# Moving two pairs of SBUF buffers by 192 bytes in a two-block transformer kernel

## The chip, the cores and the metric

The kernel is one program on one core of a Trainium2 chip. The metric is device time in microseconds (us) of one execution; lower is better. The times given are medians of several executions.

## The reference

Two transformer blocks work on 256 tokens of width 1024, in float32. The first has a gated feed-forward (inner width 2816), a mixer with two branches (a spatial gating unit and a stick-breaking attention of 16 heads), and a second gated feed-forward. The second has two attention layers, each followed by an MLP of inner width 4096. Nearly all arithmetic is the product of a 256-row activation with a weight that is streamed once from HBM:

```
def swiglu(x, w_gate, w_up, w_down):
    return (jax.nn.silu(x @ w_gate) * (x @ w_up)) @ w_down
...
def squared_relu_mlp(x, w_up, w_down):
    return jnp.square(jax.nn.relu(x @ w_up)) @ w_down
...
        h = h + merge_heads(mix) @ w_o[layer]
        h = h + squared_relu_mlp(rms_norm(h, mlp_norm[layer]), w_up[layer], w_down[layer])
```

## The kernel before

**Weights.** SyncE issues all weight loads in a fixed order, in units of 128 x 1024 (or 128 x 512) floats, into the ring `raw` (6 slots). For each unit ScalarE writes a rounded copy `w_hi` (L633) and VectorE the remainder `w_lo` (L985), both of type float32r, in rings of 8 slots. TensorE multiplies three times for one product: low activation by high weight, high by high, high by low (the helper `three`, L1479).

**Activations.** They are split in the same way. `xt` holds the normalized input, transposed, with high and low parts interleaved; `yt_hi`, `yt_lo` hold the attention outputs and other 1024-wide operands; `ht_hi`, `ht_lo` hold the inner activations of a feed-forward chunk. The chunks of a feed-forward alternate: even ones use `ht`, odd ones use `yt` (`h_buffers`).

**Two forms of matmul.** In the first (the up projections at L1568, L1570, L1575, and the projections to queries and keys at L1479) the weight is loaded as the stationary operand and `xt` is streamed, 256 columns. In the second (the down projections and all products that leave rows of tokens, L1479) the activation is loaded as the stationary operand, 128 columns, and the weight is streamed, 512 columns. Each matmul has its own weight load (LDWEIGHTS, "PEld" in the profile), which TensorE does while the matmul before it streams. `yt` and `ht` are only ever loaded as stationary operands in the second form; the one exception is the stick-breaking attention, where `ht` holds a triangular cumulative sum's input and is streamed (L1712, L1715).

**Where buffers lie.** SBUF tensors are placed one behind another in each partition. A filler `gap_in` of 192 bytes stands ahead of `xt`, and a filler `gap_out` of 64 bytes behind `ht_lo`. All the sizes between are multiples of 256 bytes, so modulo 256 the starts are: `raw`, `w_hi`, `w_lo`, `x`, `side` at 128; `xt`, `yt`, `ht` at 64; `work`, `qt`, `kt`, `vn`, the constants at 128. Every operand's offset inside its buffer is a multiple of 512 bytes for the matmuls of the two forms. So, modulo 256, in the second form the streamed weight starts 64 bytes past the stationary activation, and in the first form the streamed `xt` starts 192 bytes past the stationary weight.

**Order.** Each engine's instructions are written out by hand and joined by semaphores. The lines the prediction speaks of are these:

```
        gap_in = sb("gap_in", [P, 48])
        xt = sb("xt", [P, KT, 2, S], F32R)
...
        yt_hi = sb("yt_hi", [P, KT, S], F32R)
...
                for n, (p, q) in enumerate(((a[1], b[0]), (a[0], b[0]), (a[0], b[1]))):
                    ins = pe.matmul(dst, p, q, start=first and n == 0, stop=last and n == 2)
```

Of the kernel before, what the change touches and what calls it, by code (L numbers as in the profile page):

```python
# [25 lines left out]
P = 128  # L26
# [117 lines left out]
def two_blocks(nc, x_in, ff1_norm, ff1_w_gate, ff1_w_up, ff1_w_down, mix_norm, w_in, b_gate, gmlp_ln_g,  # L144
# [4 lines left out]
    with ctx:  # L149
        def sb(name, shape, dt=F32, scope=ctx):  # L150
            return scope.enter_context(nc.sbuf_tensor(name, shape, dt))
# [10 lines left out]
        gap_in = sb("gap_in", [P, 48])  # L162
        xt = sb("xt", [P, KT, 2, S], F32R)
        xt_hi, xt_lo = xt[:, :, 0, :], xt[:, :, 1, :]
        yt_hi = sb("yt_hi", [P, KT, S], F32R)
        yt_lo = sb("yt_lo", [P, KT, S], F32R)
        ht_hi = sb("ht_hi", [P, 4, S], F32R)
        ht_lo = sb("ht_lo", [P, 4, S], F32R)
        gap_out = sb("gap_out", [P, 16])
        work = [sb(f"work{n}", [P, 2, 512]) for n in range(3)]  # L170
        ws = side[:, 0, 0:GROUPS * P].rearrange("p (g s) -> p g s", g=GROUPS)
        qt = sb("qt", [P, 2, S])
# [1816 lines left out]
```

How the kernel before makes its waits and increments, by code:

```python
        def consumed(eng, c, i=0):  # L303
            eng.wait_ge(s["used"], RING + c + 1 + RING * i)
# [4 lines left out]
        @block.sync  # L310
# [1 line left out]
            def room(c, i):  # L312
                sp.wait_ge(s["lo_ready"], RING + c - RAW + 1 + RING * i)
# [67 lines left out]
            def norm_rows():  # L382
                sp.wait_ge(s["sp_done"], HEADS)
                sp.wait_ge(s["r_ready"], HEADS)
                for row, dst in zip((gmlp_ln_g, gmlp_ln_b), ln_rows):
                    sp.dma_start(dst, row.rearrange("a g c -> a (g c)").broadcast_to([P, D])).then_inc(s["blk1_in"], 16)
# [64 lines left out]
            proj_units("w_out", wout, lambda i: 0)  # L452
            ff_units("ff2", ff2_w_gate, ff2_w_up, ff2_w_down)
            att_units("moba", *qkv_moba)
            out_units("w_o0", wo[0])
            mlp_units("mlp0", w_up_2[0], w_down_2[0])
            att_units("fox", *qkv_fox)
            out_units("w_o1", wo[1])
            mlp_units("mlp1", w_up_2[1], w_down_2[1])
            for tok in range(TOK):
                sp.wait_ge(s["second_out"], tok + 1)
                sp.dma_start(out[0, tok * P:(tok + 1) * P, 512:D], side[:, tok, 512:D]).then_inc(s["stored"], 16)
            sp.wait_ge(s["stored"], 32 * TOK)
# [6 lines left out]
            def const(ins, name="const_done"):  # L471
                ins.then_inc(s[name], 1)
                count["n"] += 1
                pool.wait_ge(s[name], count["n"])
# [95 lines left out]
            def pairs(phase):  # L571
                if phase == "fox":
                    pool.wait_ge(s["cn_done"], 1)
                if phase != "stick":
```

## Time and profile before

| | |
|---|---|
| median of 3 runs | 1219.84 us (1215.82 to 1220.4) |
| the profiled execution | 1215.18 us, of which the span of its instructions 1213.4 us |
| TensorE matmul busy | 99% of the span |
| VectorE, ScalarE, GpSimd busy | 65%, 52%, 7% |
| granted TensorE clock | 0.999 of full speed |
| DMA | 183 GB/s in the mean |

A matmul's busy time in the profile is its duration from first column to last result; matmuls overlap, so what a matmul costs is the distance from its start to the next start, which is read from the timeline.

### The profile page before, as it was taken

The numbers are of one execution on the slowest core, as the hardware profiler recorded it, in microseconds if no ns is written. First come the engines' busy times: TensorE is split into PE (matmuls) and PEld (weight loads), VectorE is DVE, ScalarE is ACT, GpSimd is POOL, SyncE is SP. The second block draws the span as 40 slices with busy tenths as digits, with TensorE's granted clock in tenths as the row PEclk, the third lists the DMA queues.
The fourth block names the chain that finished last, engine by engine and source line by source line (L and its number), as shares of the span: only waits on it lengthen the run. The fifth ranks groups of instructions, "written<-read, shape, count | busy, mean of one in ns | idle before, by whom it ended". The sixth has DMA issues, their size and how long they took to land.

```text
span 1213.4 us, 19913 instructions
## 1 busy us (share of the span) xinstructions
PE 1204.6 (99%) x8039; PEld 1080.2 (89%) x8039; DVE 784.9 (65%) x1189; ACT 629.2 (52%) x965; POOL 90.2 (7%) x192
## 2 busy tenths in 40 slices
PE   9999999999999999999999999999999999999998
PEld 9999998998888889999988889989888888999896
DVE  6666656576576666666666777865646676866654
ACT  6544436666544346444455666444437465744443
POOL 2000000221000010000003210000000550000000
PEclk9999999999999999999999999999999999999999
DMA  8865566645664557666565445866654654676640
GB/s 261 259 191 185 183 199 191 184 128 186 217 208 139 182 155 221 200 199 187 176 194 158 138 140 181 272 200 195 185 166 119 171 163 157 213 249 196 192 141 35
DMA packets 174907, 221.88 MB, mean 183 GB/s; under 512 B 9268, under 2 KB 103568, under 8 KB 174816
## 3 DMA queue, kind: packets, MB, share of 16 engines
q1 hardware_dynamic: 173264, 217.09, 57.5%
q0 software_dynamic: 1248, 3.00, 0.9%
q8 instruction: 63, 1.03, 0.3%
q10 hardware_dynamic: 304, 0.53, 0.1%
q14 instruction: 28, 0.23, 0.1%
HBM read 219.52 MB, written 1.06 MB: 182 GB/s over the span
## 4 chain that ended last, share of the span: by engine, by line
PE 98%; DVE 1%; ACT 0%; issue 0%; POOL 0%; POOLq 0%; ACTq 0%; DVEq 0%
PE bank L1479 57%; PE bank L1570 11%; PE bank L1568 11%; PE bank L1575 11%; PE bank L1500 1%; PE bank L1738 1%; PE bank L1721 1%; PE bank L1698 1%; PE bank L1696 1%; PE bank L1742 0%; DVE w_lo L985 0%; PE bank L1930 0%; PE bank L1712 0%; PE bank L1689 0%; PE bank L1535 0%
## 5 line engine op out<-in xcount | busy, mean ns | idle before, releaser
L985 DVE TENSOR_TENSOR w_lo<-raw,w_hi 128x1024 fp32r<-128x1024 f32 (+1 forms) x448 | 492.7, 1119 | 252.6 <-ACT w_hi L633 251.3
L633 ACT ACTIVATE w_hi<-raw 128x1024 fp32r<-128x1024 f32 (+1 forms) x448 | 426.0, 974 | 323.2 <-PE bank L1575 208.4
L1568 PE MATMUL bank<-xt,w_hi 128*128 128x256 f32 x1216 | 304.6, 277 | 0.5 <-ACT w_hi L633 0.5
L1570 PE MATMUL bank<-xt,w_hi 128*128 128x256 f32 x1216 | 304.2, 277 | 0.0
L1568 PEld LDWEIGHTS bank<-xt,w_hi 128*128 128x128 f32 x1216 | 228.3, 188 | 2.1 <-ACT w_hi L633 0.8
L1570 PEld LDWEIGHTS bank<-xt,w_hi 128*128 128x128 f32 x1216 | 228.4, 188 | 1.4
L1575 PE MATMUL bank<-xt,w_lo 128*128 128x256 f32 x1216 | 229.4, 276 | 0.0
L1575 PEld LDWEIGHTS bank<-xt,w_lo 128*128 128x128 f32 x1216 | 179.8, 188 | 0.0
L1479 PE MATMUL bank<-w_hi,xt 128*128 128x512 f32 x512 | 160.3, 394 | 0.0
L1479 PE MATMUL bank<-w_lo,yt_hi 128*128 128x512 f32 x336 | 132.4, 394 | 0.0
L1479 PE MATMUL bank<-w_hi,yt_lo 128*128 128x512 f32 x336 | 132.2, 393 | 0.0
L1479 PE MATMUL bank<-w_hi,yt_hi 128*128 128x512 f32 x336 | 131.7, 392 | 0.0
L1479 PEld LDWEIGHTS bank<-w_hi,xt 128*128 128x128 f32 x512 | 94.8, 188 | 22.3 <-issue 2.1
L1479 PE MATMUL bank<-xt,w_hi 128*128 128x256 f32 x640 | 110.6, 277 | 0.0
L1479 PE MATMUL bank<-w_lo,xt 128*128 128x512 f32 x256 | 100.5, 393 | 0.0
L1479 PEld LDWEIGHTS bank<-xt,w_hi 128*128 128x128 f32 x640 | 96.6, 188 | 0.2
L1479 PE MATMUL bank<-xt,w_lo 128*128 128x256 f32 x320 | 90.0, 281 | 0.0
L1479 PE MATMUL bank<-w_lo,ht_hi 128*128 128x512 f32 x224 | 88.3, 394 | 0.0
L1479 PE MATMUL bank<-w_hi,ht_hi 128*128 128x512 f32 x224 | 87.8, 392 | 0.0
L1479 PE MATMUL bank<-w_hi,ht_lo 128*128 128x512 f32 x224 | 87.2, 389 | 0.0
L1479 PEld LDWEIGHTS bank<-w_hi,yt_lo 128*128 128x128 f32 x336 | 63.1, 188 | 13.8 <-issue 1.0
L1479 PEld LDWEIGHTS bank<-w_hi,yt_hi 128*128 128x128 f32 x336 | 63.1, 188 | 13.3
(214 smaller groups left out, 1249.1 us busy)
## 6 DMA issues: line engine op xcount, KB each, us to landing
raw<-in_w_up SPq DMA_DIRECT2D x64, 512.0 KB, 4.2
raw<-in_w_down SPq DMA_DIRECT2D x64, 512.0 KB, 4.9
raw<-in_w_in SPq DMA_DIRECT2D x56, 512.0 KB, 4.8
raw<-in_ff_w_gate SPq DMA_DIRECT2D x88, 256.0 KB, 3.7
raw<-in_ff_w_up SPq DMA_DIRECT2D x88, 256.0 KB, 4.3
raw<-in_ff_w_down SPq DMA_DIRECT2D x88, 256.0 KB, 3.8
raw<-in_moba_w_qkv SPq DMA_DIRECT2D x24, 512.0 KB, 4.0
raw<-in_w_o SPq DMA_DIRECT2D x16, 512.0 KB, 4.0
```

The source lines that it names most:

```text
L633: act.activation(w_hi[:, c % RING, 0:w], raw[:, c % RAW, 0:w], ACT.Copy).then_inc(s["hi_ready"], 1)
L985: dve.tensor_tensor(w_lo[:, c % RING, 0:w], raw[:, c % RAW, 0:w], w_hi[:, c % RING, 0:w].bitcast(F32), ALU.subtract).then_inc(s["lo_ready" ...
L1479: ins = pe.matmul(dst, p, q, start=first and n == 0, stop=last and n == 2)
L1500: ins = pe.transpose(turn_place(phase, k)[:, tok * P:(tok + 1) * P], src[:, tok, k * P:(k + 1) * P], ident[:])
L1568: pe.matmul(up_place(m, q), w, xt_hi[:, k, :], start=k == 0 and q % 2 == 0, stop=False, skip_group_check=True)
L1570: pe.matmul(up_place(m, q), w, xt_lo[:, k, :], start=False, stop=False, skip_group_check=True)
L1575: ins = pe.matmul(up_place(m, q), w_l[:, k % 2, q * P:(q + 1) * P], xt_hi[:, k, :], start=False, stop=k == KT - 1, skip_group_check=True)
L1696: pe.matmul(z[:, 0:P], q[:, 0:P], k[:, 0:P], start=True, stop=True)
L1698: ins = pe.matmul(z[:, P:3 * P], q[:, P:S], k[:, 0:S], start=False, stop=True, skip_group_check=True)
L1721: ins = pe.transpose(t_bank[h][:, o * P:(o + 1) * P], work[1][:, h, o * P:(o + 1) * P], ident[:])
L1738: pe.matmul(y[rows, 0:S], vn[:, e, 0, rows], work[2][:, h, 0:S], start=True, stop=False)
```

## The change

`yt_hi`, `yt_lo`, `ht_hi` and `ht_lo` start 192 bytes further on, and all that follows them starts 256 bytes further on. Modulo 256 the four lie at 0 and everything else is where it was. In the second form of matmul on `yt` and `ht` the streamed weight then starts 128 bytes past the stationary activation. No instruction is added, removed or reordered on any engine.

```diff
         xt = sb("xt", [P, KT, 2, S], F32R)
         xt_hi, xt_lo = xt[:, :, 0, :], xt[:, :, 1, :]
+        gap_mid = sb("gap_mid", [P, 48])
         yt_hi = sb("yt_hi", [P, KT, S], F32R)
         yt_lo = sb("yt_lo", [P, KT, S], F32R)
         ht_hi = sb("ht_hi", [P, 4, S], F32R)
         ht_lo = sb("ht_lo", [P, 4, S], F32R)
-        gap_out = sb("gap_out", [P, 16])
+        gap_out = sb("gap_out", [P, 32])
```

## Rows read from the trace of the kernel before

**Rows 1.** The page: span, busy time of each engine, chain by engine and line.

```profile
span 1213.4 us, 19913 instructions
...
PE 1204.6 (99%) x8039; PEld 1080.2 (89%) x8039; DVE 784.9 (65%) x1189; ACT 629.2 (52%) x965; POOL 90.2 (7%) x192
...
PE 98%; DVE 1%; ACT 0%; issue 0%; POOL 0%; POOLq 0%; ACTq 0%; DVEq 0%
PE bank L1479 57%; PE bank L1570 11%; PE bank L1568 11%; PE bank L1575 11%; PE bank L1500 1%; PE bank L1738 1%; PE bank L1721 1%; PE bank L1698 1%; PE bank L1696 1%; PE bank L1742 0%; DVE w_lo L985 0%; PE bank L1930 0%; PE bank L1712 0%; PE
```

**Rows 2.** Span and granted TensorE clock of the core.

```profile
core 0: 1213.4 us, clock 0.999
```

**Rows 3.** Tile `yt_hi`: duration ns min/median/max, first and last start us.

```profile
L1479 PE MATMUL bank<-w_hi,yt_hi x336: 387/392/399, 48.4 to 1206.9; 128*128 128x512 f32 x168
...
L1479 PE MATMUL bank<-w_lo,yt_hi x336: 388/394/398, 48.7 to 1207.1; 128*128 128x512 f32 x168
L705 ACT ACTIVATE yt_hi<-work x26: 614/617/635, 38.1 to 1187.9; 128x512 fp32r<-128x512 f32 x26
L1066 DVE TENSOR_TENSOR yt_lo<-work,yt_hi x26: 682/685/691, 39.2 to 1189.5; 128x512 fp32r<-128x512 f32 x26
```

**Rows 4.** Tiles `yt_lo` and `ht_lo`, the same columns.

```profile
L1479 PE MATMUL bank<-w_hi,yt_lo x336: 387/388/580, 48.2 to 1206.7; 128*128 128x512 f32 x168
...
L1479 PE MATMUL bank<-w_hi,ht_lo x224: 387/388/478, 31.8 to 1195.7; 128*128 128x512 f32 x112
```

**Rows 5.** Timeline of TensorE (start us, us, what), one down projection's beginning and end.

```profile
47.97 0.39 PE L1575 MATMUL bank<-xt,w_lo 128*128 128x256 f32 x2
48.20 0.39 PE L1479 MATMUL bank<-w_hi,yt_lo 128*128 128x512 f32 x1
48.42 0.39 PE L1479 MATMUL bank<-w_hi,yt_hi 128*128 128x512 f32 x1
48.65 0.39 PE L1479 MATMUL bank<-w_lo,yt_hi 128*128 128x512 f32 x1
48.88 0.39 PE L1479 MATMUL bank<-w_hi,yt_lo 128*128 128x512 f32 x1
...
53.46 0.39 PE L1479 MATMUL bank<-w_lo,yt_hi 128*128 128x512 f32 x1
53.69 0.28 PE L1568 MATMUL bank<-xt,w_hi 128*128 128x256 f32 x1
```

**Rows 6.** Timeline of TensorE, the end of the up projection that follows.

```profile
64.37 0.39 PE L1575 MATMUL bank<-xt,w_lo 128*128 128x256 f32 x2
64.59 0.39 PE L1479 MATMUL bank<-w_hi,ht_lo 128*128 128x512 f32 x1
```

**Rows 7.** Timeline of TensorE in another up projection, sixteen matmuls apart.

```profile
18.33 0.28 PE L1568 MATMUL bank<-xt,w_hi 128*128 128x256 f32 x1
...
20.21 0.40 PE L1575 MATMUL bank<-xt,w_lo 128*128 128x256 f32 x2
```

**Rows 8.** Timeline of TensorE after eight transposes in a product on `yt`.

```profile
386.98 0.48 PE L1479 MATMUL bank<-w_hi,yt_lo 128*128 128x512 f32 x1
387.29 0.40 PE L1479 MATMUL bank<-w_hi,yt_hi 128*128 128x512 f32 x1
387.53 0.39 PE L1479 MATMUL bank<-w_lo,yt_hi 128*128 128x512 f32 x1
387.76 0.39 PE L1479 MATMUL bank<-w_hi,yt_lo 128*128 128x512 f32 x1
```

**Rows 9.** Timeline of TensorE: plain float32 matmuls of 256 columns, six of them.

```profile
371.73 1.46 PE L1930 MATMUL bank<-a_uv,wst 128*128 128x256 f32 x6
```

**Rows 10.** Tile `ht_hi` as streamed operand; the page's costliest ScalarE and VectorE groups.

```profile
L1712 PE MATMUL bank<-ht_hi,ntri_r x16: 332/363/391, 226.8 to 290.2; 128*128 128x384 f32 x16
...
L985 DVE TENSOR_TENSOR w_lo<-raw,w_hi 128x1024 fp32r<-128x1024 f32 (+1 forms) x448 | 492.7, 1119 | 252.6 <-ACT w_hi L633 251.3
L633 ACT ACTIVATE w_hi<-raw 128x1024 fp32r<-128x1024 f32 (+1 forms) x448 | 426.0, 974 | 323.2 <-PE bank L1575 208.4
```

## The prediction, made before the changed kernel was run

> **What bounds the kernel now.** I read the page first: TensorE is busy 99% of the 1213.4 us span, and the chain that ended last is 98% TensorE, with no other engine above 1% [rows 1]. The granted clock is 0.999 of full speed, the 2.4 GHz level, all the time [rows 2]. So the kernel is one row of matmuls, and its time is their number times the distance from one start to the next. ScalarE waits 323.2 us and VectorE 252.6 us ahead of their conversions of weights, most of ScalarE's for TensorE [rows 10]: they have room, and a faster TensorE would not run into them at once. This matters in both directions: whatever the change does to a matmul's spacing comes out in the time one for one.
>
> Next the spacing, from the timeline. In the down projection shown, 24 matmuls of 512 columns start between 48.20 and 53.69 [rows 5], which is 5.49 / 24 = 0.2288 us each. The up projection that follows has 96 matmuls of 256 columns between 53.69 and 64.59 [rows 5, 6]: 10.90 / 96 = 0.1135 us each. At 2.4 GHz the columns alone take 512 / 2.4 = 213.3 ns and 256 / 2.4 = 106.7 ns. So a matmul with 512 streamed columns pays 15.5 ns above its columns, and one with 256 pays 6.8 ns. Plain float32 matmuls, which spend two clocks on a column, show almost none of it: six of 256 columns take 1.46 us, less 0.38 us for the last one's own length, over five distances = 216 ns, against 213.3 [rows 9]. The excess therefore belongs to float32r operands at one column per clock. That is what a change of addresses could touch.
>
> **The change, part by part.**
>
> *Matmuls on `yt` and `ht` as stationary operands.* There are 336 in each of three kinds on `yt` (low by high, high by high, high by low) and 224 in each of three on `ht` [rows 3, 4]: 3 x 336 + 3 x 224 = 1680. At 228.8 ns they take 384 us, 32% of the span. Only these change their relation: the streamed weight goes from 64 to 128 bytes past the stationary activation, modulo 256. The 512-column matmuls on `xt` and all those with 256 columns keep theirs. One nanosecond of spacing on the 1680 is 1.68 us, 0.14% of the time.
>
> The relation of 128 bytes occurs in no stretch of the profile of any weight, so its price has to be bounded from the rows at hand.
> - Below: the whole excess vanishes but for what the plain float32 matmuls show (216 ns): (228.8 - 216) x 1680 = 21.5 us less.
> - A nearer lower bound: twice the spacing of the 256-column form, 227.0 ns, which has another relation (192): 1.8 x 1680 = 3.0 us less.
> - Above: the 256-column form has a second, slower pace at the same relation. Sixteen matmuls from 18.33 to 20.21 take 1.88 us, 117.5 ns each [rows 7]. Twice that is 235.0. And the 512-column form shows a value like it for one matmul after an interruption, 387.29 to 387.53, before it falls back to about 230 [rows 8]. A lasting 235 would cost 6.2 x 1680 = 10.4 us more.
>
> I take zero. The reason is a test that the trace makes by itself at the seams between the forms. The last matmul of the up projection streams `xt` (at 64) while `yt_lo` (also at 64) is loaded for the next: the two lie 0 apart, not 192. Both of the merged pair and the step into the down projection take 48.20 - 47.97 = 0.23 us for two, as everywhere [rows 5]; the pair ahead of `ht_lo` takes 64.59 - 64.37 = 0.22 [rows 6]. The last matmul of the down projection streams `w_lo` while a slice of `w_hi` is loaded, again 0 apart instead of 64: 53.69 - 53.46 = 0.23 us, as everywhere [rows 5]. So the distances 0 and 64, and 0 and 192, cost the same to within the 10 ns of the display, and I see no reason in these rows for 128 to be the odd one. The weakness is plain: a single matmul in a steady row may not show what a lasting relation would, and 10 ns is most of the excess.
>
> The Trainium skill, page "SBUF — State Buffer", section "Who interferes with whom", says that TensorE has two independent read ports, one for the moving operand and one for the weight load, and never waits on anyone. By that rule the sum is zero whatever the rows say; rows 7, with two paces at equal addresses, show that something it does not describe does hold the stream up. The page "TensorE: Matmul & The Clock Gate", section "Back-to-back issue gap", gives N / 2.4 + 2.5 ns for a warm matmul, 215.8 ns at 512 columns. The trace agrees for the plain float32 matmuls (216) and not for the float32r ones (228.8); by that formula the most that could be won is 13.0 x 1680 = 21.8 us.
>
> *Where `ht` is streamed.* In the stick-breaking attention 16 matmuls of 384 columns stream `ht_hi`, with durations from 332 to 391 ns [rows 10], and as many stream `ht_lo`. If each of 32 moved by the whole width of that, 59 ns, it would be 1.9 us; they wait for VectorE there anyway. I take zero, bounds of 1.9 us either way.
>
> *Writers of the four buffers.* ScalarE writes a chunk's high part in 617 ns and VectorE the low part in 685 ns, with 9 ns between VectorE's smallest and largest [rows 3]. Their destination moves from 64 to 0 modulo 256. There are 26 of each on `yt` [rows 3], so some 54 with those on `ht`, as the chunks alternate, and they are done while TensorE is in the next chunk's up projection, 10.90 us long, which hides a doubling. Without that cover, a tenth more on each would be 54 x 0.13 = 7 us. I take zero.
>
> *The rest* moves by 256 bytes and keeps its place modulo 256: zero.
>
> Sum: 1213.4 us span, no term. The profiled execution took 1215.18 us, the median of the three timed ones is 1219.84 us, 0.4% above it. Measurements are against the median, so the sum gives 1219.8; the small lower bound of 3.0 us is likelier than any equal rise, and I forecast 1218.5.
>
> **The rivals.**
>
> *A. The excess of the 512-column form is partly a collision of two read streams, and 128 bytes apart is clear of it.* For it: 15.5 ns of excess is more than twice the 6.8 of the 256-column form, though in both the same 128-column load runs beside the stream; the forms differ in relation (64 against 192). If the load beside the stream costs the 512-column form what separates the paces of the 256-column form, 117.5 - 113.5 = 4.0 ns [rows 5 to 7], and that goes, it is 4.0 x 1680 = 6.7 us: 1213.1 us. If the load's whole share goes and only the stream's length counts, the spacing falls towards 220, 8.8 x 1680 = 14.8 us: 1205.0 us. Against it: the seams. Something over 6 us is needed to be told from no change.
>
> *B. Slower: 128 bytes apart holds the row of matmuls in the slower pace.* The mechanism is the second pace of rows 7, in the place of the down projections and the output products. Rows 8 show that at a relation of 64 the stream leaves a start at 240 ns and settles below 230; a relation at which it settled at 235 would give the 10.4 us of above: 1230.2 us. It decides from 3.6 ns a matmul upward (6.1 us). For it: at one relation two paces exist, so relations may well differ in which they settle at, and 228.8 is nearer to twice the fast pace (227.0) than to twice the slow one (235.0), so there is more room above than near below. Against it: nothing at a relation of 0 or 64 stays slow for long.
>
> *C. The relation does change the pace, but by less than 3.6 ns*, either way. This ends where the forecast does.
>
> **How the numbers follow.** What a measurement of this kernel can tell from no change is about 0.5%, 6.1 us. Forecast and C together: 0.38. A: 0.36. B: 0.26. As these three cases are the three signs, they are also the chances: faster 0.36, same 0.38, slower 0.26. The range must leave out no more than 2 in 10: below, it takes in A's nearer case and most of the way to its farther one, and leaves out the disappearance of all excess; above, it takes in B at 235 with a little for spread: 1203 to 1231. The likeliest case alone would be 1214 to 1225.
>
> **What the profile of the changed kernel would show.** The 24 matmuls of the down projection that began at 48.20 should again take 5.49 us; under A 5.39 or less (5.28 at 220 ns), under B about 5.64. The 96 matmuls after it should take 10.90 us in all cases, and the matmuls on `xt` with 512 columns should keep 228.8 ns. The medians of 388, 392 and 394 ns of the three kinds on `yt` should be unchanged. The prediction is wrong if the spacing of the 1680 moves by more than 3.6 ns, or if the spacing of matmuls that keep their relation moves at all, which would mean that addresses matter in some other way than modulo 256.

## The result, and the profile after

The changed kernel takes 1226.80 us (median of 5 runs, 1225.85 to 1227.25); the kernel before, on the same chip, took 1219.84 (5 runs, 1215.82 to 1220.42). The ratio over all runs of both is 1.007 (the two medians alone give 1.0057), with a 95% interval of 1.0052 to 1.0087: slower by 0.7%, and clear of no change. The forecast of 1218.5 and "no change" was wrong; the time lies inside the range given.

Span and clock, and the rows of the page that answer to [rows 1, 2, 10]:

```profile
span 1224.1 us, 19913 instructions
...
PE 1215.4 (99%) x8039; PEld 1085.8 (89%) x8039; DVE 785.0 (64%) x1189; ACT 629.0 (51%) x965; POOL 90.5 (7%) x192
...
PE 99%; ACT 0%; DVE 0%; issue 0%; POOL 0%; POOLq 0%; ACTq 0%; DVEq 0%
...
L986 DVE TENSOR_TENSOR w_lo<-raw,w_hi 128x1024 fp32r<-128x1024 f32 (+1 forms) x448 | 492.7, 1118 | 260.9 <-ACT w_hi L634 258.9
L634 ACT ACTIVATE w_hi<-raw 128x1024 fp32r<-128x1024 f32 (+1 forms) x448 | 425.8, 974 | 332.4 <-PE bank L1576 212.3
```

```profile
core 0: 1224.1 us, clock 0.999
```

The span grew by 10.7 us at the same clock. VectorE and ScalarE work as long as before and wait 8.3 and 9.2 us longer: the time was added on TensorE, and everyone else waits for it. Every line behind L165 is one higher than before.

The tile `yt_hi`, and `yt_lo`, as in [rows 3, 4] (duration ns min/median/max):

```profile
L1480 PE MATMUL bank<-w_hi,yt_hi x336: 387/393/404, 48.4 to 1217.6; 128*128 128x512 f32 x168
...
L1480 PE MATMUL bank<-w_lo,yt_hi x336: 389/393/404, 48.6 to 1217.9; 128*128 128x512 f32 x168
L706 ACT ACTIVATE yt_hi<-work x26: 612/618/636, 37.9 to 1198.2; 128x512 fp32r<-128x512 f32 x26
L1067 DVE TENSOR_TENSOR yt_lo<-work,yt_hi x26: 681/685/687, 39.0 to 1199.9; 128x512 fp32r<-128x512 f32 x26
```

```profile
L1480 PE MATMUL bank<-w_hi,yt_lo x336: 388/393/582, 48.1 to 1217.4; 128*128 128x512 f32 x168
```

The writers are unmoved. The three kinds of matmul, at 388, 392 and 394 before, are all at 393. Then the timeline of TensorE (start us, us, what) in the places of [rows 5, 6], and from one chunk of the first MLP:

```profile
48.15 0.39 PE L1480 MATMUL bank<-w_hi,yt_lo 128*128 128x512 f32 x1
...
53.72 0.28 PE L1569 MATMUL bank<-xt,w_hi 128*128 128x256 f32 x1
...
64.61 0.39 PE L1480 MATMUL bank<-w_hi,ht_lo 128*128 128x512 f32 x1
...
787.19 0.39 PE L1480 MATMUL bank<-w_hi,yt_lo 128*128 128x512 f32 x1
...
798.34 0.28 PE L1569 MATMUL bank<-xt,w_hi 128*128 128x256 f32 x1
...
809.65 0.39 PE L1480 MATMUL bank<-w_hi,ht_lo 128*128 128x512 f32 x1
```

In the feed-forward the down projection takes 5.57 us for 24 matmuls, 232.1 ns each, against 228.8; the up projection 10.89 / 96 = 113.4, as before. In the MLP the down projection of 48 takes 11.15 us, 232.3 ns each, and here the up projection, whose addresses modulo 256 did not move, takes 11.31 / 96 = 117.8. The same one before:

```profile
794.88 0.28 PE L1568 MATMUL bank<-xt,w_hi 128*128 128x256 f32 x1
...
805.79 0.39 PE L1479 MATMUL bank<-w_hi,ht_lo 128*128 128x512 f32 x1
```

That is 10.91 / 96 = 113.6. So there are two parts. For means over all matmuls of a kind I took the distances between start times in the trace, leaving out those over 260 ns (512 columns) or 150 ns (256 columns), which are interruptions: the 1680 on `yt` and `ht` went from 229.0 to 232.3 ns, 5.6 us; the 1534 distances in the up projections of the two MLPs from 113.6 to 117.2, 5.6 us; the 2104 in the two gated feed-forwards gained 0.3 us back; everything else stayed. Together 10.9 us, of 10.7 measured. All means are of one profiled execution of each kernel; the spans of the four other executions of the changed kernel, 1224.5 to 1225.5 us, agree with its 1224.1.

### The profile page after: what moved, and what is told of

Same layout as the page of the kernel before. It is cut to its first block, busy times and chain, and to the rows that moved or that the text cites. A ratio compares the mean times of both kernels' runs of the same rounds, so it can differ in the third digit from the quotient of the medians.

```text
span 1224.1 us, 19913 instructions
## 1 busy us (share of the span) xinstructions
PE 1215.4 (99%) x8039; PEld 1085.8 (89%) x8039; DVE 785.0 (64%) x1189; ACT 629.0 (51%) x965; POOL 90.5 (7%) x192
## 4 chain that ended last, share of the span: by engine, by line
PE 99%; ACT 0%; DVE 0%; issue 0%; POOL 0%; POOLq 0%; ACTq 0%; DVEq 0%
PE bank L1480 57%; PE bank L1569 11%; PE bank L1571 11%; PE bank L1576 11%; PE bank L1501 1%; PE bank L1739 1%; PE bank L1722 1%; PE bank L1699 1%; PE bank L1697 1%; PE bank L1713 0%; PE bank L1743 0%; PE bank L1690 0%; PE bank L1931 0%; PE bank L1716 0%; PE bank L1536 0%
## 5 line engine op out<-in xcount | busy, mean ns | idle before, releaser
L1569 PEld LDWEIGHTS bank<-xt,w_hi 128*128 128x128 f32 x1216 | 229.1, 188 | 2.2 <-ACT w_hi L634 0.8
L1480 PEld LDWEIGHTS bank<-w_lo,yt_hi 128*128 128x128 f32 x336 | 63.2, 188 | 14.8
```

Of the source, the lines that this page charges most:

```text
L1569: pe.matmul(up_place(m, q), w, xt_hi[:, k, :], start=k == 0 and q % 2 == 0, stop=False, skip_group_check=True)
```

## Experiments

The theory after the result: the distance between float32r matmuls depends on where the streamed operand starts relative to the one loaded as stationary, modulo 256 (called the relation below), and 128 is worse than 64. In every run the weights stay at 128 modulo 256 and only the other operand moves, so a relation is here always also a place of `xt`, `yt` or `ht` modulo 256: which of the two counts is not separated by these runs, and "relation" is used as a name for both. The rivals: it is the position alone, or any move; only one of the two tiles matters (the matmul's own stationary one, or the one being loaded beside the stream); and, for the up projections, that something is handed on across a seam, either by the relation of the matmuls ahead or by the phase in which they leave. "Seam" is the step from one form to the other. All edits but two change fillers only.

**Moved by 256 bytes instead of 192** (against before). All four buffers move, no relation changes.

```diff
+        gap_mid = sb("gap_mid", [P, 64])
```

> yt and ht lie 256 bytes further on and everything behind them too, so that every start is where it was modulo 256. Theory R (the relation of streamed weight and stationary activation modulo 256 sets the spacing): spacing of the 512-column matmuls on yt and ht 228.9 ns, up projections 113.4 to 113.6 ns, time as before within 0.3%. Rival P (what counts is the absolute place, or the relation to something further than 256 bytes): spacing near 232.4 ns, and the up projections of the two MLPs near 117.8 ns, time about 1226 us.

Measured: 1216.47 us, the kernel before 1216.49, ratio 1.0001 (0.9991 to 1.001). `yt` and `ht` at 229.0 ns, MLP up projections at 113.6. Having moved is not the cause; what counts repeats after 256 bytes. One stage differs in the profiled execution: the 336 matmuls of 512 columns on `xt` from 295.38 us on are at 233.2 ns, against 229.0 before, with every start where it was modulo 256. That is a second, slower pace of the 512-column form at relation 64, and it makes most of the 2.2 us by which this span is longer than that of before.

**Only `ht` moved** (against before).

```diff
         yt_lo = sb("yt_lo", [P, KT, S], F32R)
+        gap_ht = sb("gap_ht", [P, 48])
...
-        gap_out = sb("gap_out", [P, 16])
+        gap_out = sb("gap_out", [P, 32])
```

> Only ht_hi and ht_lo move by 192 bytes; yt stays. The chunks alternate between ht and yt. Theory R: down projections on ht 232.4 ns, on yt 228.9 ns. Theory S (the slow pace of an up projection is handed on by the down projection ahead of it): in the MLPs the up projections behind a down on ht run at 117.8 ns, those behind a down on yt at 113.6 ns, which gives about half of the rise, 3 of 5.5 us on the down projections and 2 to 3 of 5.5 us on the up ones, 1218 to 1219 us for the profiled execution. Rival: the up projections slow down for another reason (what the whole layout does), then all or none of them at 117.8 ns.

Measured: 1222.73 us, ratio 1.0056 (1.0039 to 1.0073). `ht` 232.2 ns, `yt` 229.2: here the new relation acts on just the matmuls that have it, 3.3 x 672 = 2.2 us. The MLP up projections are at 116.7 in the mean, 4.8 us. Not every other one, as the relation of the down projection ahead would have it, but all from the third chunk on, also this one, behind a down projection on `yt`:

```profile
796.69 0.28 PE L1569 MATMUL bank<-xt,w_hi 128*128 128x256 f32 x1
...
807.99 0.39 PE L1480 MATMUL bank<-w_hi,ht_lo 128*128 128x512 f32 x1
```

11.30 / 96 = 117.7 ns. A slow pace, once there, outlives a down projection whose relation is the old one. That spoke for a phase handed on.

**Relation 192 on `yt` and `ht`, and relation 0** (against before; moved by 128 and by 64 bytes).

```diff
+        gap_mid = sb("gap_mid", [P, 32])
...
-        gap_out = sb("gap_out", [P, 16])
+        gap_out = sb("gap_out", [P, 48])
```

```diff
+        gap_mid = sb("gap_mid", [P, 16])
...
-        gap_out = sb("gap_out", [P, 16])
+        gap_out = sb("gap_out", [P, 64])
```

> yt and ht moved by 128 bytes: the streamed weight lies 192 bytes past them (64 bytes ahead). Theory R in its simple form (a collision that depends on distance alone, the same on both sides): as the kernel before, 228.9 ns. Theory R with direction: another spacing of its own, between 227 (twice that of the 256-column form, which has this relation) and 238. Rival P: 228.9 to 232.4, no pattern.

> yt and ht moved by 64 bytes: the streamed weight lies 0 past them. If the relation matters as a collision of two reads in equal places, this is the worst: over 232.4 ns, a time over 1227 us. If the seams of the trace before told the truth (0 as good as 64), it is 228.9 ns and the time of before.

Measured: 192 gives 1229.14 us, ratio 1.0107 (1.0092 to 1.0122); 0 gives 1225.99, ratio 1.0082 (1.0067 to 1.0097). Timeline at 192:

```profile
781.78 0.28 PE L1569 MATMUL bank<-xt,w_hi 128*128 128x256 f32 x1
...
793.09 0.39 PE L1480 MATMUL bank<-w_hi,yt_lo 128*128 128x512 f32 x1
...
804.29 0.28 PE L1569 MATMUL bank<-xt,w_hi 128*128 128x256 f32 x1
...
815.19 0.39 PE L1480 MATMUL bank<-w_hi,ht_lo 128*128 128x512 f32 x1
```

The down projection takes 11.20 / 48 = 233.3 ns a matmul. The up projection ahead of it takes 11.31 us, the one behind it 10.90: the two paces of 256 columns, in turn, at one set of addresses. Timeline at 0:

```profile
49.01 0.39 PE L1480 MATMUL bank<-w_hi,yt_lo 128*128 128x512 f32 x1
...
54.45 0.28 PE L1569 MATMUL bank<-xt,w_hi 128*128 128x256 f32 x1
...
802.02 0.28 PE L1569 MATMUL bank<-xt,w_hi 128*128 128x256 f32 x1
...
813.33 0.39 PE L1480 MATMUL bank<-w_hi,ht_lo 128*128 128x512 f32 x1
```

5.44 / 24 = 226.7 ns (227.0 in the mean of all 1680): the fastest that any relation gave, two nanoseconds under before. It had been expected to be the worst, over 232.4, or as good as 64. But every up projection of 96 behind a down projection is at 11.31 us, 117.8 ns, and in the sum (-3.3 us on the 1680, +7.6 in the gated feed-forwards, +6.5 in the MLPs) it costs 10.8, of 11.0 measured in the span.

**`xt` moved as well: relations of the 256-column form** (against before; `yt` and `ht` stay at 64 in all but the first). `gap_in` goes from 192 to 0, 128, 64, 160 and 224 bytes, and `gap_mid` puts `yt` back where it was (not in the first, where all is at relation 0).

The edit for relation 128:

```diff
-        gap_in = sb("gap_in", [P, 48])
+        gap_in = sb("gap_in", [P, 32])
...
+        gap_mid = sb("gap_mid", [P, 16])
```

> No gap ahead of xt: xt, yt, ht and the weights all start at the same place modulo 256, so the relation is 0 in both forms. Theory R: down projections and the products on xt at 226.7 ns, as yt and ht showed at relation 0. The 256-column form has not been seen at relation 0: if it is bound to the same law, an even pace of about 113.4 ns, and the kernel comes under the one before by (228.9 - 226.7) x 2424 = 5.3 us; if its slow pace is the steady one there, 117.8 ns on 4800 matmuls, 15 us or more above it.

> xt is 128 bytes away from the weights in both forms, yt and ht stay at relation 64. Theory R: products on xt with 512 columns at 232 to 233 ns; those on yt and ht at 228.9. The pace of the 256-column form at relation 128 is open: between 113.4 and 120. If it is 117.8 throughout, the time is near 1233 us.

> xt lies 64 bytes past the weights: relation 64 in the 256-column form, 192 in the 512-column form on xt. Theory R: the latter at 233.3 ns (as yt and ht at 192); yt and ht at 228.9. If the law of the 512-column form holds for the 256-column one, relation 64 is between 0 and 128 and gives a pace not far from 114.5.

> xt moved by -32 bytes: relation 160 in the 256-column form (192: two paces, 113.4 and 117.8; 128: about 120), yt and ht stay at 64. Smooth law: between 115 and 119, and the time up by 10 us or more. Law of whole lines: as 128 or as 192. On xt with 512 columns the relation becomes 96.

> xt moved by 32 bytes: relation 224 in the 256-column form (192: 113.4 or 117.8; 0: 120), yt and ht stay at 64. If 192 is the bottom of a smooth law, slower than before; if the bottom lies between 192 and 256, the slow pace is gone and some matmuls come under 113.4. On xt with 512 columns the relation becomes 32, between 226.7 and 228.9 ns.

**32 bytes off on `yt` and `ht`** (against before; `gap_mid` of 32 bytes, relation 32).

> yt and ht moved by 32 bytes: relation 32, halfway between 0 (226.7 ns, the up projections slow) and 64 (228.9 ns, fast). If the spacing follows the distance smoothly: 227.8 ns, 1.8 us less on the 1680. If it counts whole lines of 64 bytes: as one of the two neighbours, exactly. Together with up projections at 113.4 it would be the first to beat the kernel before, at 1213 to 1214 us; with up projections at 117.8, 1226 us.

The six together, mean distances in ns (in each the relation of the 256-column form, of the 512-column form on `xt`, and of that on `yt` and `ht`):

| relations | time us, ratio (95%) | up projections | 512 on `xt` | 512 on `yt`, `ht` |
|---|---|---|---|---|
| 0, 0, 0 | 1240.70, 1.0197 (1.0172 to 1.0223) | 119.9 | 227.7 | 227.5 |
| 128, 128, 64 | 1245.14, 1.0233 (1.0207 to 1.0259) | 119.8 | 232.5 | 229.3 |
| 64, 192, 64 | 1237.76, 1.0173 (1.0147 to 1.0198) | 117.7 | 233.3 | 229.2 |
| 160, 96, 64 | 1240.88, 1.0205 (1.0188 to 1.0222) | 118.6 | 233.4 | 229.2 |
| 224, 32, 64 | 1239.67, 1.0195 (1.0178 to 1.0212) | 118.3 | 233.2 | 229.0 |
| 192, 64, 32 | 1236.57, 1.0170 (1.0155 to 1.0185) | 117.5 | 229.3 | 233.3 |

The 512-column form is at 229 at relation 64 and at 233 at 32 and 192, on `xt` as on `yt` and `ht` (96 was run on `xt` alone): it belongs to the relation, not the buffer. It is not smooth in the distance: 32 is worse than 0 and than 64, where 227.8 or one of the neighbours' values had been expected. No other relation of the 256-column form has the pace of 113.4 for long: at 64 one row of 24 matmuls, from 18.09 us on, is at 113.4 and the rest at 117.8; at 0, 128, 160 and 224 no 24 matmuls of the up projections are under 117. With 32 on `yt` and `ht` every up projection of 96 behind a down projection is slow at an unchanged 192.

**One transpose of 128 columns ahead of twelve MLP up projections** (against the changed kernel; one short matmul added at the seam, its result is overwritten).

```diff
+                        if j == 0 and m > 1 and not gated:
+                            pe.transpose(up_place(m, 0)[:, 0:P], ident[:], ident[:])
```

> The changed kernel, and in the two MLPs, from the third chunk on, one transpose of the unit matrix into the bank that the up projection is about to overwrite, between the down projection and the up projection behind it (12 in all). It breaks the row of float32r matmuls at the seam. Theory S (the down projection hands its phase to the up projection, which keeps it to its end): each of the ten up projections at 117.8 ns gets a new phase, and some or all run at 113.4 to 113.6; up to 10 x 96 x 4.2 = 4.0 us less, and 12 x 0.2 = 2.4 us more for the transposes. Rival T (the relation of yt and ht makes the up projections slow in another way, say through the engines that write them): all stay at 117.8 ns and the time rises by 2.4 us.

Measured: 1225.80 us, ratio to before 1.0072 (1.0046 to 1.0098). With it, in two chunks that follow each other:

```profile
777.28 0.37 PE L1571 MATMUL bank<-xt,w_hi 128*128 128x256 f32 x1
...
788.25 0.39 PE L1480 MATMUL bank<-w_hi,yt_lo 128*128 128x512 f32 x1
...
799.43 0.36 PE L1571 MATMUL bank<-xt,w_hi 128*128 128x256 f32 x1
...
810.82 0.39 PE L1480 MATMUL bank<-w_hi,ht_lo 128*128 128x512 f32 x1
```

10.97 and 11.39 us, each with one long first distance (206 and 201 ns): 113.4 and 117.8 for the rest. Eight of the twelve up projections behind a transpose are fast now, where two of these twelve were, 115.6 in the mean of both MLPs, at the addresses of the changed kernel. Of the gain, 1534 x 1.6 = 2.5 us, the twelve transposes take 12 x 0.11 = 1.3 us (an entry of 201 to 207 ns for one of 118, and some 25 ns for the transpose itself), and what is left is too small to be told in the time.

**Only the low parts at 128** (against before; fillers that put `yt_lo` and `ht_lo` 192 bytes on and the high parts back).

```diff
+        gap_a = sb("gap_a", [P, 48])
         yt_lo = sb("yt_lo", [P, KT, S], F32R)
+        gap_b = sb("gap_b", [P, 16])
         ht_hi = sb("ht_hi", [P, 4, S], F32R)
+        gap_c = sb("gap_c", [P, 48])
         ht_lo = sb("ht_lo", [P, 4, S], F32R)
-        gap_out = sb("gap_out", [P, 16])
+        gap_out = sb("gap_out", [P, 32])
```

> Only yt_lo and ht_lo lie 128 bytes from the streamed weight, yt_hi and ht_hi stay at 64. Each product is low by high weight, high by high, high by low. Theory L (what collides is the stream with the load of the next stationary operand, beside it): the matmuls that stream w_lo and load a low part beside them pay, those that stream w_hi on a low part do not. Theory O (it is the relation to the operand already loaded): the other way round. Either way the mean over the three lies between 228.9 and 232.4, near 230, and the time between 1217 and 1226 us; if the up projections of the MLPs are handed the slow pace, 5 us more than if not.

Measured: 1219.62 us, ratio 1.003 (1.0019 to 1.0041). The 1680 are at 231.6 ns, 4.4 us of the 4.2 that the span grew, with a third of the stationary tiles moved; the MLP up projections stay at 113.5. By kind: low by high 232.5, high by high 231.1, high by low 231.1 (before 226.3, 229.1, 231.5). Two kinds changed, one of them with its own stationary tile where it was. So a matmul is not alone in paying for its relation, and this run does not separate the tile in use from the tile being loaded.

**The kernel before with the same twelve transposes** (against before; no address changed), **and relation 0 in parts**: both high parts, both low parts, or `yt` alone (the fillers are of the same kind).

> The kernel before, with one transpose of 128 columns put ahead of each of the same twelve up projections as in the seam run, and no address changed. What phase alone does: if a break at the seam can throw an up projection into the slow pace whatever the addresses of yt and ht, some of the twelve show 117.8 ns a matmul, each worth 96 x 4.2 = 0.4 us, up to 4.8 us for twelve. If the pace is decided by the relation that the matmuls ahead of the seam had, which is 64 here as in the kernel before, all twelve keep 113.6, and the time rises by the transposes alone, 12 x 0.1 to 0.2 = 1.2 to 2.4 us, within 0.2% of the kernel before.

> yt_hi and ht_hi lie 0 from the streamed weights, yt_lo and ht_lo stay at 64. Two of each three matmuls stream past a stationary tile at 0, where a lasting relation of 0 gave 226.7 ns. If spacing is set by the matmul's own stationary tile or by the one loaded beside it alike, the mean of the 1680 is about (2 x 226.7 + 228.9) / 3 = 227.4, 2.5 us less. Up projections: if the relation 0 of the last matmuls is what sends them into the slow pace, the MLP ones show 117.8 (+5 us or more, 1219 to 1226 us); if it is the relation of the low part, loaded first in each three, they stay at 113.6 and the time is 1213 to 1215 us.

> The other half: yt_lo and ht_lo at 0, the high parts at 64. One in three matmuls has relation 0: mean about 228.2, 1.2 us less. If the low part's relation decides the pace of the up projections, they show 117.8 here and 113.6 in the run with the high parts at 0; if the high part's does, the other way round; if both must be 0, both runs keep 113.6.

> Both parts of yt at 0, both of ht at 64. The 1008 matmuls on yt fall to about 226.8 (2.2 us less), the 672 on ht stay at 228.9. Up projections that follow a down projection on yt: if the pace is handed on at each seam anew, those are at 117.8 and those behind ht at 113.6, half of 5 us or more lost (1217 to 1220 us). If a slow pace once entered stays, as when ht alone lay 128 apart, all from the third chunk on are slow (1220 to 1225 us).

Measured, mean distances in ns again:

| kernel | time us, ratio (95%) | up, gated | up, MLP | on `ht`, `yt` |
|---|---|---|---|---|
| transposes alone | 1221.71, 1.0052 (1.0038 to 1.0065) | 113.9, 117.4 | 115.6 | 229.8, 229.6 |
| high 0, low 64 | 1218.94, 1.0024 (1.0015 to 1.0033) | 114.0, 113.6 | 113.6 | 231.1, 231.1 |
| high 64, low 0 | 1228.40, 1.0101 (1.0088 to 1.0114) | 117.1, 117.4 | 116.7 | 229.1, 229.3 |
| `yt` 0, `ht` 64 | 1226.61, 1.0088 (1.0075 to 1.0101) | 116.7, 117.0 | 117.2 | 230.0, 227.2 |

The transposes settle the main point: eight of the twelve up projections behind them are at 117.8, with every relation as in the kernel before. In the five other executions, whose spans lie 4 to 5 us above that of a typical run of before, eight slow rows and twelve transposes make 8 x 0.4 + 12 x 0.11 = 4.5 us.

Of relation 0 in parts: high parts at 0 give 231.1 where 227.4 was expected, and leave the MLP up projections fast; low parts at 0 give 229.2 where 228.2 was expected, and make most of them slow. That is what "the low part's relation decides the pace" had forecast for the up projections, but since the transposes change the pace with no relation changed, it can be no more than one way to set what is handed on. By kind, the run with the high parts at 0 has low by high, whose own tile did not move, at 233.6 (before 226.3), so neither the own tile nor the next one alone sets a distance. `yt` at 0 went nearly as the second of its two cases: slow from the fourth chunk of each feed-forward on, the first behind `yt`, and from there also behind `ht` at 64.

And the transposes show two things that were not asked. Their profiled execution has a slow row of up projections in the second gated feed-forward, ahead of the first of the transposes, where the program is that of the kernel before, instruction for instruction. Timeline there:

```profile
475.91 0.28 PE L1570 MATMUL bank<-xt,w_hi 128*128 128x256 f32 x1
...
487.22 0.40 PE L1479 MATMUL bank<-w_hi,yt_lo 128*128 128x512 f32 x1
487.46 0.39 PE L1479 MATMUL bank<-w_hi,yt_hi 128*128 128x512 f32 x1
...
492.73 0.28 PE L1570 MATMUL bank<-xt,w_hi 128*128 128x256 f32 x1
```

and the same up projection of the kernel before:

```profile
474.69 0.28 PE L1568 MATMUL bank<-xt,w_hi 128*128 128x256 f32 x1
...
485.60 0.39 PE L1479 MATMUL bank<-w_hi,yt_lo 128*128 128x512 f32 x1
```

11.31 against 10.91 us: one program, one clock, two paces, and all nine up projections behind the first slow one are slow too. Over the 1053 distances this is 4.0 us. That execution had a span of 1223.7 us, the five others 1218.8 to 1219.7; that these others were fast in that place is inferred from their spans. The up projection ahead of this one, with which the slow row begins, is slow in the changed kernel with transposes too (11.39 us from 460.20, against 10.98 in the changed kernel), again ahead of the first transpose. Second, a down projection at relation 64 can have another pace as well:

```profile
856.07 0.40 PE L1479 MATMUL bank<-w_hi,ht_lo 128*128 128x512 f32 x1
...
867.27 0.27 PE L1565 MATMUL bank<-ident 128*128 128x128 f32 x1
```

11.20 / 48 = 233.3 ns, where the kernel before has 228.9. It is the pace that one stage had in the run moved by 256 bytes.

What is handed on can be seen in the single distances, which repeat in short cycles. In ns, from the trace's start times:

```
down projection (end of it)        next up projection
before        226 229 231 226 229 231 | 118 116 118 122 119 113 ... 113 114 113   fast
transposes,
2nd gated     229 232 225 230 231 227 | 117 118 118 118 117 119 ... 118 117 119   slow
high 64 low 0 226 229 231 229 232 227 | 117 118 118 117 118 118 ... 117 118 118   slow
relation 0    227 227 226 227 227 226 | 118 117 119 117 118 118 ... 118 117 118   slow
after, gated  233 241 232 231 232 233 | 120 116 114 113 114 113 ... 113 114 113   fast
after, MLP    231 231 229 230 232 234 | 118 117 119 117 118 118 ... 117 118 118   slow
```

In the first two rows the relation is 64 and the cycle is the same, 226, 229, 232, but shifted by one matmul. I counted the up projections of 96 that follow directly on a settled cycle at relation 64, in before and in the runs moved by 256 bytes, with `ht` alone moved, with `yt` at 0, and with the transposes alone. Of those behind a cycle that leaves with 230 to 232, 78 of 78 are fast; of those behind one that leaves with 226 or 227, 27 of 27 are slow. They are not 105 independent trials, since each loop repeats itself. In 32 of 39 cases a slow up projection starts the next down projection at relation 64 with 235, 231, 237, 232, 231, then the cycle, which shifts it and makes the next up projection slow: the slow loop keeps itself, as the fast one does, at the same addresses. In the other 7 it starts with 236 and stays at 233.3 ns, and the three up projections that follow such a row directly are fast.

At relation 128 the cycle has seven matmuls: 241 232 231 232 228 230 233, in the changed kernel and with `ht` alone moved. The down projection of a gated feed-forward has 24 matmuls, three cycles and three; that of an MLP has 48, six cycles and six. So they leave at different places. Behind the 24, four distances after the last 241, 27 of 27 up projections of 96 are fast; behind the 48, six or seven distances after it, 16 of 16 are slow. (Three more follow a down projection that kept 229 and 238 by turns, and are fast.) This is why the MLPs of the changed kernel are slow and its gated feed-forwards are not, as far as the trace tells it.

## Why the prediction was wrong

*What bounds the kernel* held: the row of matmuls is the kernel, and 10.9 us of summed distances appeared as 10.7 us of span.

*"I take zero. The reason is a test that the trace makes by itself at the seams."* This is the step that failed. A lasting relation of 192 gives the 512-column form 233.3 ns, of 32 or 96 the same, of 128 232.3 and of 0 227.0, where the test had said that 0, 64 and 192 cost the same. The weakness named there was real: what differs is a cycle of several matmuls (three at relation 64, seven at 128), one matmul at a seam does not show it, and a display in steps of 10 ns hides an effect of 2 to 4 in one distance. The rule cited from the Trainium skill, page "SBUF — State Buffer", section "Who interferes with whom", by which TensorE never waits on anyone, gave the same zero; the run moved by 256 bytes (ratio 1.0001) beside the one moved by 192 (1.007) goes against this zero for float32r operands.

*Rival B* named the direction and the kind, a relation that holds the matmuls at a slower distance. Its price was that of 235.0 ns, 6.2 x 1680 = 10.4 us; measured were 3.3 x 1680 = 5.6 us. By itself that is under the 3.6 ns from which B was to decide, and so case C. That the time still came out near B's, and inside the range, is luck: it is the other 5.6 us, of which B knew nothing.

*"The 96 matmuls after it should take 10.90 us in all cases"* failed in the MLPs, 11.31, and no term of the sum or bound held it. The row was at hand: [rows 7] showed the slow pace at unchanged addresses. I used it as a price for the 512-column form and not as what it is, a state into which the 256-column form can be put by what runs ahead of it. Priced on all 3638 distances of the up projections it is 4.2 ns, 15.3 us, more than the 10.4 us of rival B. What the prediction named for this case, "that addresses matter in some other way than modulo 256", is not what it means either: the move by 256 bytes changed nothing, and the transposes alone changed the pace.

*Rival A* had the right thought, that some relation is better than 64, and the wrong relation: 0 gives 227.0 ns. The nearer lower bound in the prediction, 227.0, is that value, by chance: it was taken from the 256-column form at 192, and the 512-column form at 192 has 233.3.

*The small terms.* The conversions of chunks (618 and 685 ns) and the streamed `ht` moved by nothing that counts, as taken. The medians of 388, 392 and 394 ns were to stay and became 393 each: the first sign in the trace, since a duration that depends on the kind of matmul is the cycle, seen in another view.

*The median of before.* It was 1219.84 here and 1215.7 to 1216.5 in the later comparisons; its five runs fall into 1215.8 to 1215.9 and 1219.8 to 1220.4, and of the 44 later ones two are at 1219.6 to 1219.7. Against 1216.5 the change costs 10.3 us, near the 10.7 of the spans, and not 7.0. One gated feed-forward in the slow loop is 4.0 us, which would be this gap. It was shown in one execution of the transposes' kernel, not in one of the kernel before, so for the latter it is argued.

**What stays open.** Whether it is the relation or the place modulo 256 of the operand that moved: a run with the weights moved and `xt`, `yt`, `ht` left where they are would tell, and none was made. Why the cycles are what they are, and which of the two stationary tiles counts: the runs with one part moved give 231.6 (low at 128), 231.1 (high at 0) and 229.2 (low at 0), which no rule of one tile explains. What sets the first row of a feed-forward, behind no down projection, is open too: it is slow in some executions and fast in others. Relation 0 with fast up projections would be, as an estimate from the sum above, 3.3 us under before; no run had both, and none tried a seam that brings it about. No kernel here beats the kernel before.

## What to carry to other kernels

Where a row of float32r matmuls is the whole time, its distance depends on addresses (up to 2.3% of this kernel's time) and on what ran ahead: try the four or so relations modulo 256 (a filler of 64 bytes each) and measure, since neither order nor smoothness helps to guess. Take the mean distance of every form and stage from start times, not only of the matmuls that changed: neighbours with unchanged addresses can move by as much. A second pace seen anywhere in the trace is a term of the sum: multiply it by all the matmuls that could fall into it, and when a kernel's times fall into two groups, look there too.

## What the runs showed of the hardware that I had not expected

- Distance of float32r matmuls, 512 columns streamed past a loaded tile of 128: 227.0 to 227.7 ns at relation 0 (226.7 in a settled row), 229.0 at 64 (233.3 in some rows), 231.9 to 233.3 at 128 by row, 233.3 at 32, 96 and 192. With 256 columns: 113.4 or 117.8 at 192, 117.7 at 64 (113.4 in one row of 24), 118.3 at 224, 118.6 at 160, 119.8 at 128 and 119.9 at 0. The best relation of one form is the worst of the other. All with the weights at 128 modulo 256.
- The distances repeat in cycles, of three matmuls at relation 64 (226, 229, 232) and of seven at 128, and the place in the cycle at which one stage ends goes with the pace of the next, 105 times of 105 at relation 64 and 43 of 43 at 128.
- One short matmul at a seam moves a stage from one pace to the other, worth 0.4 us for 96 matmuls; one execution had the other pace ahead of any change in the program. At relation 64 the stages behind mostly stay there.
